# Late pool columns and late gates moved, five re-orderings kept, in a two-layer kernel fed by row gathers

## The reference, cut to what matters

```python
def block(xb):                                   # 128 tokens
    q = (xb @ w_q).reshape(128, 8, 2, 128)
    s1 = einsum("thd,hnd->thn", q[:, :, 0], k1); s2 = ...
    v1, i1 = top_k(s1, 16); v2, i2 = top_k(s2, 16)
    ...
    idx = take_along_axis(cand_i, pos, axis=-1)  # 16 experts a head
    g = softmax(top_s, axis=-1)
    u = down[idx]
    act = gelu(einsum("thkd,td->thk", u, xb))
    return einsum("thk,thkd->td", g * act, up[idx])
```

## Time and profile before

| what | value |
| --- | --- |
| median of 3 runs | 3172.35 us |
| the profiled execution's own time | 3180.19 us |
| its span | 3178.7 us |
| TensorE clock granted, mean share | 0.977 |
| PE, DVE, ACT, POOL busy | 82%, 64%, 39%, 34% of the span |
| rows gathered | 1024, from 433.5 us to about 3150 us |
| HBM read | 1175.48 MB, 370 GB/s over the span |

### The profile page before, as it was taken

How to read it: one execution, slowest core, us unless ns; L and a number is a source line. 1 busy time by engine, 2 the same in 40 slices (tenths; PEclk the granted TensorE clock), 3 DMA queues, 4 the chain that set the end, 5 groups by cost and what they waited for, 6 DMA issues and landing times.

```text
span 3178.7 us, 35977 instructions
## 1 busy us (share of the span) xinstructions
PE 2592.5 (82%) x12092; PEld 1075.0 (34%) x12092; DVE 2023.8 (64%) x5008; ACT 1229.0 (39%) x3892; POOL 1078.4 (34%) x1041
## 2 busy tenths in 40 slices
PE   7999988777877877778988878887777877988777
PEld 3555643323322323223332344333222332322111
DVE  4532447777777777665554756677777776765544
ACT  3122324544434444334223443444343543444323
POOL 0000014433434343334433333344443434343431
PEclk9999999999999999999999999999999999999999
DMA  9411349999999999999999999999999999999996
GB/s 357 149 53 53 120 185 374 421 420 420 417 421 421 419 404 415 418 418 416 416 414 417 406 408 390 416 420 418 421 421 420 408 421 413 417 420 420 399 421 263
DMA packets 198780, 1179.94 MB, mean 371 GB/s; under 512 B 20994, under 2 KB 21700, under 8 KB 67268
## 3 DMA queue, kind: packets, MB, share of 16 engines
q0 software_dynamic: 147456, 1073.81, 81.8%
q1 hardware_dynamic: 51140, 103.84, 8.9%
HBM read 1175.48 MB, written 2.10 MB: 370 GB/s over the span
## 4 chain that ended last, share of the span: by engine, by line
DMA 51%; PE 31%; ACT 6%; DVE 5%; issue 4%; POOL 3%; SPq 0%; another core or an unknown queue 0%; DVEq 0%; POOLq 0%; ACTq 0%
DMA scr<-in_peer_rows,idx_v 20%; PE banks L814 20%; DMA scr<-in_expert_rows,idx_v 12%; DMA ring<-in_expert_rows,idx_v 11%; PE banks L1166 10%; DMA ring<-in_peer_rows,idx_v 5%; DVE scr L2275 2%; POOL ring L788 2%; POOL scr L788 1%; DMA scr<-in_w_in 1%; ACT ring L1664 1%; DVE ring L2275 1%; ACT L1658 1%; ACT L1620 1%; ACT scr L1658 1%
## 5 line engine op out<-in xcount | busy, mean ns | idle before, releaser
L1166 PE MATMUL banks<-scr,ring 128*32 128x512 f32 x2080 | 861.1, 609 | 213.5 <-ACT ring L1664 198.0
L1166 PE MATMUL banks<-ring 128*32 128x512 f32 x2016 | 797.2, 628 | 247.4 <-ACT ring L1664 231.2
L2275 DVE CUSTOM_DVE_ANT_0 ring<-ring 128x1024 f32<-128x1024 f32 x502 | 615.3, 1226 | 415.7 <-DMA ring<-in_expert_rows,idx_v 218.2
L1658 ACT ACTIVATE scr<-scr 128x1 f32<-128x1 f32 x1024 | 206.7, 202 | 1491.7 <-DVE scr L2275 1475.1
L2275 DVE CUSTOM_DVE_ANT_0 scr<-scr,banks 128x1024 f32<-128x1024 f32 x254 | 310.1, 1221 | 221.5 <-DMA scr<-in_peer_rows,idx_v 115.5
L2275 DVE CUSTOM_DVE_ANT_0 scr<-scr,ring 128x1024 f32<-128x1024 f32 x266 | 325.9, 1225 | 194.5 <-DMA scr<-in_peer_rows,idx_v 104.4
L788 POOL DMA_INDIRECT ring<-in_peer_rows,idx_v x248 | 261.1, 1053 | 535.3 <-PE banks L1166 492.8
L814 PE MATMUL banks<-hT,scr 128*128 128x128 f32 (+3 forms) x2576 | 374.7, 306 | 66.3 <-DVE ring L2257 45.6
L1166 PEld LDWEIGHTS banks<-scr,ring 128*32 128x32 f32 x2080 | 171.5, 110 | 756.5 <-ACT ring L1664 446.1
L788 POOL DMA_INDIRECT scr<-in_expert_rows,idx_v x256 | 274.9, 1074 | 427.5 <-PE banks L1166 393.1
L1166 PEld LDWEIGHTS banks<-ring 128*32 128x32 f32 x2016 | 159.1, 112 | 731.2 <-ACT ring L1664 442.3
(11 more groups left out here) (255 smaller groups left out, 2179.4 us busy)
## 6 DMA issues: line engine op xcount, KB each, us to landing
scr<-in_w_in SPq DMA_DIRECT2D x8, 2048.0 KB, 28.7
scr<-in_w_mod SPq DMA_DIRECT2D x7, 2048.0 KB, 11.0
ring<-in_w_in SPq DMA_DIRECT2D x7, 2048.0 KB, 12.7
scr<-in_w_q SPq DMA_DIRECT2D x6, 2048.0 KB, 39.1
ring<-in_w_mod SPq DMA_DIRECT2D x5, 2048.0 KB, 12.8
scr<-in_peer_w_q SPq DMA_DIRECT2D x4, 2048.0 KB, 11.5
scr<-in_peer_rows,idx_v POOLq DMA_INDIRECT x264
ring<-in_w_out SPq DMA_DIRECT2D x2, 2048.0 KB, 7.7
```

What stands on the lines that cost most here:

```text
L1166: last = nc.tensor.matmul(psum[2 + c][32 * g:32 * g + 32, :], spread[:, i % 8, :], rows[slot_of(i)][:, D + c * CW:D + (c + 1) * CW], start ...
L1658: nc.scalar.activation(gelu[:, h, k:k + 1], dots[:, h, k:k + 1], ACT.Gelu if i < N_ROWS else ACT.Gelu_apprx_tanh).then_inc(gelu_done, 1)
L2275: V.tensor_tensor_reduce(u, u, xq[g], 1.0, 0.0, ALU.mult, ALU.add, dots[:, n % 2, k:k + 1]).then_inc(dotted, 1)
```

## The change

Five re-orderings, and what depends on them:

1. The two extra slots come into use at row 38 instead of row 36, and the later cycle of slots is 2, 3, 0, 1, 4, 5, 6, 7. Rows 36 and 37 go to slots 6 and 7.
2. At the start PE adds pair 2 (rows 4 and 5) ahead of the moves of head 1's indices and gates instead of behind them.
3. The second-half projection of tile 2 by `w_out` is at pairs 8 and 10 instead of 9 and 11 (tile 3 stays at 13 and 15).
4. Projections `wo2` are cut into halves of 4 k-steps at neighbouring pairs (`project_2_part`).
5. `gate(2, 0)` and `gate(2, 1)` at pairs 465 and 467 become four half steps at 464, 466, 468 and 470; ACT's `gates(2)` goes from 467 to 471, `products(2)` from 469 to 472, and what follows later likewise.

In the late part `puL` goes from pair 269 to 270, `late_gates` from 271 to 274, `late_pools` from 277 to 278; ACT's `late_u` from 271 to 272, `late_rows` from 278 to 279; DVE's four late steps from rows 547 to 551 to rows 551 to 554.

```diff
-OPENING = 36
+OPENING = 38
-    return (2, 3, 6, 7, 0, 1, 4, 5)[(i - OPENING) % SLOTS]
+    return (2, 3, 0, 1, 4, 5, 6, 7)[(i - OPENING) % SLOTS]
...
+                add_pair(2)
                 move_idx(1)
                 move_gate(1)
-                add_pair(2)
...
-                      264: first_late_cols, 266: lambda: late_cols("cvL", 2, 5), 269: lambda: late_cols("puL", 3, 4),
-                      271: late_gates, 277: late_pools, 279: lambda: tile_rows("gf", 1),
-                      282: lambda: project_2(2, 0), 285: lambda: project_2(2, 1), 288: lambda: project_2(3, 0),
+                      264: first_late_cols, 266: lambda: late_cols("cvL", 2, 5), 270: lambda: late_cols("puL", 3, 4),
+                      274: late_gates, 278: late_pools, 279: lambda: tile_rows("gf", 1),
+                      282: lambda: project_2_part(2, 0, 0), 283: lambda: project_2_part(2, 0, 1),
...
-            for t in (2, 3):
-                beside[4 * t + 1] = lambda t=t: project_part("wo", t, w, 0)
-                beside[4 * t + 3] = lambda t=t: project_part("wo", t, w, 1)
+            for t, first in ((2, 8), (3, 13)):
+                beside[first] = lambda t=t: project_part("wo", t, w, 0)
+                beside[first + 2] = lambda t=t: project_part("wo", t, w, 1)
...
-                      533: lambda: tile_rstd("gf", 1), 537: late_inputs, 547: late_conv, 548: late_gate, 549: late_windows,
-                      551: late_pool, 570: lambda: second(2, 0), 576: lambda: second(2, 1), 582: lambda: second(3, 0),
+                      533: lambda: tile_rstd("gf", 1), 537: late_inputs, 551: late_conv, 552: late_gate, 553: late_windows,
+                      554: late_pool, 570: lambda: second(2, 0), 576: lambda: second(2, 1), 582: lambda: second(3, 0),
```

More of the change, by code:

```diff
@@ L1363, in project_2, with project_2_part @@
                 project("wo2", t, block, (n,))
+            def project_2_part(t, n, part):
+                if part == 0:
+                    pe.wait_ge(block_in[n], 16 * 3)
+                    if t < 2:
+                        for j in range(4):
+                            empty(pe, "cb", j)
+                            empty(pe, "py", j)
+                    else:
+                        for half in range(2):
+                            empty(pe, "cbL", half)
+                            empty(pe, "pyL", half)
+                o = begin("wo2", t, n) if part == 0 else psum[jobs.bank[jobs.number("wo2", t, n)]]
+                for k in range(KT // 2 * part, KT // 2 * (part + 1)):
+                    last = mm(o[:, :], yT[:, k, t * P:(t + 1) * P], block[n][:, k, :], k, KT)
+                if part == 1:
+                    last.then_inc(bank_ready, 1)
             def next_project_2():
                 pe.wait_ge(xq_set, 3 * TT + 3)
-                project_2(1, 0)
+                project_2_part(1, 0, 0)
             def gate(t, n):
@@ L1409, in _ @@
                       234: lambda: project_2(0, 0), 236: lambda: project_2(0, 1), 240: lambda: tile_rows("gf", 0),
-                      257: next_project_2, 259: lambda: project_2(1, 1), 262: lambda: tile_rows("gm", 3),
-                      264: first_late_cols, 266: lambda: late_cols("cvL", 2, 5), 269: lambda: late_cols("puL", 3, 4),
-                      271: late_gates, 277: late_pools, 279: lambda: tile_rows("gf", 1),
-                      282: lambda: project_2(2, 0), 285: lambda: project_2(2, 1), 288: lambda: project_2(3, 0),
+                      257: next_project_2, 258: lambda: project_2_part(1, 0, 1),
+                      259: lambda: project_2_part(1, 1, 0), 260: lambda: project_2_part(1, 1, 1), 262: lambda: tile_rows("gm", 3),
+                      264: first_late_cols, 266: lambda: late_cols("cvL", 2, 5), 270: lambda: late_cols("puL", 3, 4),
+                      274: late_gates, 278: late_pools, 279: lambda: tile_rows("gf", 1),
+                      282: lambda: project_2_part(2, 0, 0), 283: lambda: project_2_part(2, 0, 1),
+                      285: lambda: project_2_part(2, 1, 0), 286: lambda: project_2_part(2, 1, 1),
+                      288: lambda: project_2_part(3, 0, 0), 289: lambda: project_2_part(3, 0, 1),
                       291: lambda: project_2(3, 1), 295: lambda: tile_rows("gf", 2), 300: lambda: tile_rows("gf", 3),
@@ L1424, in _ @@
                         beside[426 + 8 * t + 4 * n + 2 * part] = lambda t=t, n=n, part=part: gate_part(t, n, part)
+            for n in range(2):
+                for part in range(2):
+                    beside[464 + 4 * n + 2 * part] = lambda n=n, part=part: gate_part(2, n, part)
             for j in range(4):
@@ L1810, in _ @@
                       263: lambda: opening_square("wo2", "gf", 1), 264: lambda: tile_out("gm", 3, mix_gain, no_shift),
-                      265: lambda: tile_root("gf", 1), 266: late_c, 271: late_u, 278: late_rows,
+                      265: lambda: tile_root("gf", 1), 266: late_c, 272: late_u, 279: late_rows,
                       281: lambda: tile_out("gf", 1, ffn_gain, no_shift),
@@ L1820, in _ @@
                       461: lambda: tile_out("gp", 2, ple_gain, no_shift),
-                      463: lambda: gated_square(1), 465: lambda: tile_root("fin", 1), 467: lambda: gates(2),
-                      475: lambda: gated_square(2), 477: lambda: tile_root("fin", 2)}
+                      463: lambda: gated_square(1), 465: lambda: tile_root("fin", 1), 471: lambda: gates(2),
+                      478: lambda: gated_square(2), 480: lambda: tile_root("fin", 2)}
             for t in (1, 2, 3):
@@ L2501, in _ @@
                       929: lambda: tile_mean("fin", 1), 933: lambda: final(1),
-                      945: lambda: add_gated(2, 0), 947: lambda: add_gated(2, 1),
-                      953: lambda: tile_mean("fin", 2), 957: lambda: final(2)}
+                      950: lambda: add_gated(2, 0), 952: lambda: add_gated(2, 1),
+                      959: lambda: tile_mean("fin", 2), 963: lambda: final(2)}
             for t in (1, 2, 3):
```

2 lines of the change are left out of this document (1 added, 1 removed).

## The result

The changed kernel takes 3184.76 us, median of 6 runs (3183.6 to 3187.51), against 3171.78 us (3169.54 to 3178.18) for the kernel before: a ratio of 1.0039, 95% interval 1.0029 to 1.0049, or 13.0 us more. The forecast was 3175.0 us with a range of 3163 to 3185, and 3169 to 3180 as the forecast's own range.

The account below looks back on a forecast made before the run. DMA was taken as the bound from 433 us on, so terms price lost DMA time: -8.3 us from the re-orderings, +10.9 from the late part, +2.6 on the 3172.35 us median gives 3175.0 us, range 3163 to 3185.

Parts of the forecast that it names:

- The opening: Early rows: pair 2 ahead of the moves gains 2.5 us, tile 2's earlier projection 2.4, slots from row 38 1.4.
- Projections in halves: At 1820 to 1846 us, where 2.6 us are lost: gain 1.0 (0 to 2), and 0.5 for later projections.
- Gates in halves: DMA pause at 2943 to 2947 us: gain 0.5 us (0 to 1.1), not 3.3, since dots kept their pace.
- The late part: Head 36's query projection waits some 22 us for part 2 of w_q; 16.2 us lost against 5.3 before, 10.9 more.
- Rival (a): Part 2 of w_q lands in time, at about 1922 us as before; 3162.8 us; chance 0.17.
- The 5.3 us credited to before: Loss at 1918 to 1934 us, from POOL idle before the gathers of rows 548 and 552; the change removes the waits.
- DVE's catch-up: After standing in late_conv to about 1946 us, DVE does late work and search between overdue dots; gathers lose 2.5 us.
- rival (b): Waiting for query weights costs more: part 2 lands at 1935 us, DVE's catch-up takes 5 us; 3181.0 us; chance 0.18.
- The first pause: Gathers run out at about 1930 us while PE awaits part 2 of w_q, flow again at 1940.2; loss 10.2 us.
- The second pause: Gathers stop from 1945.2 to about 1951.5 us behind the late gates, weights running alone at 292 GB/s; 3.5 us lost.
- (c): The opening gives nothing because rows added sooner only meet the next wait; 3181.3 us; chance 0.15.
- The rule of the Trainium skill: VectorE with two SBUF inputs blocks GpSimd reading SBUF: 2.1 us on row 558, within the second pause, no separate term.

Follow-up runs that it names:

- late part alone: Kernel before with only the late part moved (puL, late gates, late pools, ACT and DVE steps): 3193.26 us, ratio 1.0050.
- the second queue: Changed kernel, head 36's search two pairs later, part 2 of w_q issued by ACT instead of SP, late_u at pair 271: 3168.17 us (0.9989); again 3168.10 us (0.9995).
- the slots alone: Kernel before with only the two extra slots from row 38 and the new cycle: one execution, 3168.89 us.
- query-later: Changed kernel with head 36's search two pairs later (projection at pair 276, top-k from row 556): 3169.22 us (0.9978); again 3167.07 us (0.9988).
- the gates ahead: Changed kernel with the late gates at pair 273 instead of 274, ahead of head 36's query projection: 3177.45 us, ratio 1.0003.
- the five re-orderings alone: Changed kernel with the late part at its old places: 3169.71 us, ratio 0.9979.

## Why the prediction was right or wrong

**The opening** was right: 6.3 us forecast, and by the dots 2.2 (2.5 forecast), 2.0 (2.4) and 2.4 (1.4, bounds 0 to 2). The rival that it gives nothing is out. One sign failed: POOL still idles 6.13 us before row 12's gather (6.28 before), though the gather goes out 3.8 us earlier after row 0's dot; before row 30 it idles 3.79 us, before row 36 under 2.

**Projections in halves** was wrong by 1.7 us: 1.0 gain forecast and 0.7 loss measured for rows 520 to 544, 0.5 gain forecast and some 0.5 measured later. The step that failed is that a stretch's missing GB/s are time lost. **Gates in halves** was right, 0.5 us, because there the forecast looked at the dots and not at the 76 GB/s. The same argument would have been due at 1820 us.

**The late part: the mechanism was right, step by step.** The changed trace runs 9.9 us ahead of before at row 544; add that, and its times stand beside the forecast's. PE free for the projection: 1898.5 + 9.9 = 1908.4, forecast 1908.4. Part 2 landed and PE going: 1920.96 + 9.9 = 1930.9, forecast 1930; the wait 22.47 us, forecast 22. The projection behind it took 5.33 us instead of 3.84, a restart of 1.5 us, forecast 2.4. The gathers flowing again: 1930.0 + 9.9 = 1939.9, forecast 1940.2. Rival (a), weights in time, did not come: between 1887 and 1908 us the changed kernel moved 936 packets of weights beside 926 of gathers.

**Its size was wrong.** The late part costs 286.8 - 270.2 = 16.6 us (late part alone: 289.2 - 270.2 = 19.0; 270.2 is the mean of the five kernels with old late code other than before's own profile), against a forecast of 10.9. The waits themselves were priced well: against the second queue's 269.6, where nothing waits for these weights, the changed kernel loses 17.2 us, and the forecast had 16.2. What failed is the 5.3 us set against them, and, inside the 16.2, one term was too small and another too large:

- *The 5.3 us credited to before.* That stretch of the profile was not typical. Five other executions with the old late part take 269.8 to 270.5 us from row 544 to 640 where before's profile has 272.6, and the kernel with the second queue takes 269.4 and 269.8. POOL's two idles before rows 548 and 552, 16.23 and 17.16 us in the earlier trace rows, are 33.4 us together; in the five they are 28.3 to 30.9. So the waits that the change removes cost some 0.6 us in a usual execution (estimated from 270.2 - 269.6), and 4.7 us of the credit did not exist. Nor was part 2 of `w_q` as early as the profile made it look: in three of the five PE waited 3.3 to 4.4 us for it, as here with the slots alone (the gates, then the projection):

```profile
1896.69 9.75 PE L814 MATMUL banks<-hT,scr 128*128 128x136 f32 x64 [5.30 <-DMA scr<-in_w_in]
...
1911.96 6.72 PE L814 MATMUL banks<-hT,scr 128*128 128x128 f32 x32 [3.64 <-DMA scr<-in_w_q]
```

Of the 7.8 us by which before's execution stood over the median, 2.4 lie here, and its rows began late (441.6 us; the others lie between 435.0 and 441.9).
- *DVE's catch-up*, 2.5 us forecast, is at most the 6.0 us at 1946 to 1968 (by GB/s; by POOL's two waits below, less). With late convolution, windows, pool and head 36's search between the dots, rows 552 to 563 were dotted late, PE added their slots' rows late, and POOL waited 4.84 and 4.11 us before rows 563 and 564. This is the half of rival (b) that came; its other half, a late landing, did not.

- *The first pause*, 10.2 us forecast, was right. By GB/s it is 15.3, because 15 of 16 engines ended their gathers some 5 us ahead; the last one, by which the dots go, moves its last gather at 1920.1, and the next gather moves at 1930.0: 9.9 us.
- *The second pause* was 2.0 us instead of 3.5. The forecast took 292 GB/s for weights that move alone, from a stretch that begins with a standstill; from 1923 to 1928 us they run at 386.

With these terms the late part comes to 9.9 + 2.0 + 6.0 - 0.6 = 17.3 us, beside the 16.6 and 19.0 measured. Two of its terms are still read by GB/s, so the agreement is rough.

**The total.** Forecast -8.3 + 10.9 = +2.6. Measured by the dots: -7.0 in the opening (rows 8 to 44 take 96.0 us in the mean of the eight kernels with all its edits, 103.0 in that of the three with none), +0.7 and -0.5 for the halves, +16.6 late: +9.8 us; by medians +13.0 (9.2 to 15.5). The time lies 0.2 us inside the upper end of the range, 4.8 us beyond the forecast's own range, and on the slower side, to which the text gave 0.27. That the range holds it is luck: it reached so far for rivals (b) and (c), of which (c) did not come and (b) came in part.

**The rule of the Trainium skill** (SBUF - State Buffer, "Who interferes with whom") was expected to bear on row 558. Its issue did come under the late convolution and took 2.59 us instead of 0.94 (1938.30 above). But the convolution, from 1936.69 to 1938.94, overlaps it by 0.6 us only, and in the earlier trace rows by 1.1. The dot behind it, `ring<-ring`, has two inputs in SBUF too. The issue ends 0.81 us after the end of that dot in both kernels and in the query-later ones, where it took 3.04 and 3.03 us. So the trace agrees with the rule, if the dot counts as well, and the delay depends on when the issue starts; no run takes the two apart.

**A better version** than either kernel: all the changes with head 36's search at row 556. 0.9978 and 0.9988 of the kernel before on two chips; on the first, 8.2 us below the version with the gates ahead. It ties with the five re-orderings alone (0.9979 on the first), whose late part already cost next to nothing.

## What to carry to other kernels

Moving a step behind its neighbours moves it behind their waits as well: look up what each neighbour waits for, and when that lands once the pause that let it through is gone. Price a pause of the transfers by the pace of what consumes them and by the DMA engine that is last, and not by the missing GB/s. Before a stretch of one profile is credited as a loss to be won back, look whether a second execution has it too.

## What was not expected of the hardware

- Weights beside gathers are paced by packets: 498 for 497 at 1 KB (0.051 MB/us), 1244 for 1243 at 2 KB (0.090). Halving a load's row length to get its first half sooner gains nothing. A load on another engine's queue gets a turn of its own (222 to 221 to 195 packets).
- About one of the 16 DMA engines ran some 4 us behind the others in a steady stream; at the end of the changed kernel it was alone, at 33 GB/s for 3.5 us, and from 1917 to 1920 us at 5.9% of the 16. A pause at 2943 us, 4 us at 76 GB/s, left the dots 2.48 us apart. A load is complete only with the last engine.
- One packet of gathers and one of weights in turn is seen on that lone engine too: 7 and 7.
- Executions of identical code differed by 3 us between rows 8 and 24, and in when the rows began by 7 us (435.0 to 441.9).
